# Routing by one-hot products on chip, laid inside the output projection, in an encoder layer with grouped experts

## The chip, the core and the metric

The kernel runs on one core of one Trainium2 chip. The metric is the device time of one launch in microseconds (us). Beside five engines (TensorE or PE, VectorE or DVE, ScalarE or ACT, GpSimd or POOL, SyncE or SP) the core has 16 DMA engines. SP's transfers go through one queue (q1), those that GpSimd issues, gathers and scatters by index among them, through another (q0); both use the same 16 DMA engines.

## The reference, cut to what matters

There are 768 tokens (512 and 256) of 1024 channels. A token mixer (latent attention with 4 heads beside pooling over windows) ends in a product with `w_out`; then each token goes to two of eight experts in one of four groups.

```
h = x + concat(attention, pooling) @ w_out
a = rmsnorm(h) * g_ffn
group = argmax(a @ w_group_router + b_group_router)       # 4 groups
e1, e2 = top2 of (a @ w_expert_router + b_expert_router) in that group
gate = softmax value of the group * normalised top-2 softmax values
y = h + sum over e in (e1, e2) of gate_e * (silu(a @ w_gate[e]) * (a @ w_up[e])) @ w_down[e]
```

All is float32. The 32 experts have 3 MB of weights each (1024x256, 1024x256, 256x1024), 96 MB in all, and each is read once.

## The kernel before

The program is written by hand: each engine has its own list of instructions, in the order of the code, and they meet at semaphores.

1. **Projections**, tile by tile (128 tokens, six tiles). The weights come in at the start on SP's queue, large ones first, then ten small ones (the list `small`: rotary tables, the two router matrices, broadcast gains), a slot table, two tables of zeros, and the third and fourth tile of x. DVE waits for all ten small ones (`gains_in`) ahead of the rotary tables of tile 0 (line 1065).
2. **Attention and pooling.**
3. **Output projection and routing.** For tile i, PE makes two halves of `h` (`out_half`, 24 products of 128x512 in each, lines 476 to 481). DVE adds x (line 1166). ACT squares, POOL takes the root, DVE writes the normalised row times the gain into `rows` (line 1174). PE turns the row round (`row_transposes`, line 712) and multiplies it with the router (`logits`, line 720) after the second half of the *next* tile. DVE finds the group and two experts as one-hot rows (`route`), PE counts how many earlier tokens chose each expert (`ranks`), DVE turns the counts into a place in the slot table (`positions`), and POOL writes the token's number there by an indirect DMA into memory (line 1390, two for each tile). The gates are columns 1024 to 1055 of the token's row in the table `token_rows`.
4. **Experts.** Expert j and expert 16+j form a pair; each has 64 lanes, the two halves of 128 partitions. For each of 16 pairs POOL gathers 128 rows of `token_rows` by the slot table (line 1413), PE turns them round (line 754), multiplies with gate and up weights (line 767) and with down weights (line 783), and POOL adds the 128 results to `out` (line 1432). Unused slots name a row of zeros beyond the 768. Where an expert has more than 64 tokens an *over pass* follows the pair, with its own gather (`more_rows`).

The weights of a pair come in six parts of 1 MB (gate, up, down for two lanes) into one of three buffers, on SP's queue, at most three parts under way. Part 0 to 3 of pair j are issued once PE has done gate and up of pair j-3 and of its over passes (`refill`), parts 4 and 5 once the down products are done. Ahead of the expert stage pair 0 is loaded during the output projection. Of pair 1 four parts are issued around the last tile; the other two, and pair 2, wait for the first gather (`sp.wait_ge(main.gathered[0], 16)`). The first gather waits for the slot table, which is read back (lines 426 to 429) once all 12 scatters have landed.

With the inputs of this case the experts get 1536 assignments. 1533 of the 2048 slots of the first passes are used (of pairs 0, 1 and 2 it is 110, 108 and 117 of 128); pair 0 and pair 6 have an over pass, with one and two tokens in its 128 slots. This is worked out from the reference and its inputs.

## Time and profile before

| | us |
|---|---|
| median of 3 runs | 644.66 (644.41 to 644.89) |
| the profiled execution, its own time | 643.67 |
| its span | 642.0 |
| TensorE busy | 530.8 (83% of the span) |
| VectorE, ScalarE, GpSimd busy | 223.6, 147.0, 133.2 |
| SP's queue q1 | 128.60 MB |
| GpSimd's queue q0 | 19.72 MB |

An execution is the span plus 1.7 us outside it. Line numbers in rows are those of the listing above. "PEld" is TensorE's weight load, beside PE. A row of the chain of waits is a piece of work that was followed by what waited for it; in a timeline the last bracket is how long the engine stood idle ahead of the row and what released it.

### The profile page before, as it was taken

To read this page: it belongs to the slowest core of one execution; us is meant where nothing else is said; L and a number is where in the kernel's file an instruction comes from. 1 tells how busy PE (TensorE), PEld (TensorE's weight loads), DVE (VectorE), ACT (ScalarE), POOL (GpSimd) and SP (SyncE) were. 2 spreads that over 40 slices of the span, in tenths; PEclk is the share of its full clock that TensorE was granted. 3 is DMA by queue.
4 is the path that set the end of the run, shared out by engine and by line. 5 is a ranking of instruction groups with operands and counts; after the bars stand their busy time and mean duration, and the time that the engine had idled before them with its cause. 6 is when DMAs were issued, how large, how long until landed. Compare 5 with 4: busy or idle time off the path is not lost.

```text
span 642.0 us, 8839 instructions
## 1 busy us (share of the span) xinstructions
PE 530.8 (83%) x3092; PEld 373.3 (58%) x3093; DVE 223.6 (35%) x602; ACT 147.0 (23%) x310; POOL 133.2 (21%) x200
## 2 busy tenths in 40 slices
PE   5889999997898989999725877989788897777762
PEld 4768988884444568888624545555445564434430
DVE  4743335225959562566650211121211211111110
ACT  6734343322546221121201101010100100000000
POOL 0122232032244000034323102111201232011110
PEclk9999999999999999999856989799989999889997
DMA  8730100000620039243467999999999999999992
GB/s 333 240 142 35 32 2 1 1 0 1 236 72 27 2 137 387 100 132 133 171 227 253 405 374 388 392 367 379 388 393 390 392 392 379 403 390 392 388 363 34
DMA packets 31163, 148.81 MB, mean 232 GB/s; under 512 B 7139, under 2 KB 7798, under 8 KB 18822
## 3 DMA queue, kind: packets, MB, share of 16 engines
q1 hardware_dynamic: 25376, 128.60, 50.2%
q0 software_dynamic: 5712, 19.72, 11.7%
q8 instruction: 22, 0.36, 0.2%
q14 instruction: 15, 0.12, 0.1%
q10 hardware_dynamic: 38, 0.01, 0.0%
HBM read 132.48 MB, written 17.00 MB: 233 GB/s over the span
## 4 chain that ended last, share of the span: by engine, by line
DMA 45%; PE 25%; issue 10%; DVE 6%; POOL 4%; ACT 1%; POOLq 0%; SPq 0%
DMA expert_w<-in_w_down 25%; DMA expert_w<-in_w_up 19%; PE ps L476 4%; PE ps L477 4%; PE ps L481 4%; PE ps L641 3%; POOL slot_tokens L1390 2%; PE ps L582 2%; DVE p_sb L1130 2%; PE ps L596 2%; PE ps L599 1%; PE ps L628 1%; PE ps L516 1%; DMA g_rows<-token_rows,idx_now 1%; PE ps L667 1%
## 5 line engine op out<-in xcount | busy, mean ns | idle before, releaser
L767 PE MATMUL ps<-expert_w,xT 128*64 128x256 f32 x1152 | 132.2, 386 | 16.4 <-DMA expert_w<-in_w_up 6.8
L767 PEld LDWEIGHTS ps<-expert_w,xT 128*64 128x64 f32 x1152 | 97.7, 140 | 55.5 <-issue 27.8
L783 PE MATMUL ps<-expert_w,hT 128*64 128x512 f32 x288 | 76.8, 681 | 23.7 <-DMA expert_w<-in_w_down 13.2
L1432 POOL DMA_INDIRECT out<-y_sb,idx_now x18 | 28.7, 1593 | 202.6 <-DVE y_sb L1302 201.8
L783 PEld LDWEIGHTS ps<-expert_w,hT 128*64 128x64 f32 x288 | 25.5, 155 | 63.1 <-issue 60.7
L1290 DVE SCALAR_TENSOR_TENSOR hid<-s_act,gate,ps 128x256 f32<-128x256 f32 x18 | 11.9, 660 | 141.5 <-ACT s_act L968 141.5
L476 PE MATMUL ps<-w_in_hi,aT_hi 128*128 128x384 f32 (+2 forms) x120 | 43.7, 368 | 0.0
L1302 DVE COPY y_sb<-ps 128x512 f32<-128x512 f32 x18 | 12.5, 692 | 89.5 <-PE ps L783 89.5
L477 PE MATMUL ps<-w_in_lo,aT_hi 128*128 128x384 f32 (+2 forms) x120 | 40.8, 344 | 0.0
L968 ACT ACTIVATE s_act<-ps 128x256 f32<-128x256 f32 x18 | 6.9, 384 | 133.7 <-PE ps L767 133.7
L973 ACT ACTIVATE y_sb<-ps 128x512 f32<-128x512 f32 x18 | 10.8, 597 | 105.6 <-PE ps L783 105.6
L754 PE MATMUL ps<-consts_sb,g_rows 128*128 128x128 f32 x128 | 18.4, 289 | 15.3 <-DMA g_rows<-token_rows,idx_now 15.3
L754 PEld LDWEIGHTS ps<-consts_sb,g_rows 128*128 128x128 f32 x128 | 14.4, 146 | 21.3 <-DMA g_rows<-token_rows,idx_now 16.3
L1381 POOL TENSOR_TENSOR w_out_lo<-w_out_raw,w_out_hi 128x1024 fp32r<-128x1024 f32 x8 | 19.0, 2378 | 34.1 <-ACT w_out_hi L920 34.1
L481 PE MATMUL ps<-w_in_hi,aT_lo 128*128 128x384 f32 (+2 forms) x120 | 24.3, 344 | 0.0
L477 PEld LDWEIGHTS ps<-w_in_lo,aT_hi 128*128 128x128 f32 x120 | 22.6, 188 | 2.6 <-issue 1.2
L476 PEld LDWEIGHTS ps<-w_in_hi,aT_hi 128*128 128x128 f32 x120 | 22.6, 188 | 2.6 <-issue 1.2
L582 PE MATMUL ps<-w_ukv_sb,cT_kv 128*128 128x512 f32 x48 | 21.6, 592 | 0.0
L481 PEld LDWEIGHTS ps<-w_in_hi,aT_lo 128*128 128x128 f32 x120 | 20.6, 188 | 1.6
L1390 POOL DMA_INDIRECT slot_tokens<-tok_ids,idx_pos x12 | 18.7, 1556 | 10.9 <-DVE m_sum L1246 8.3
L596 PE MATMUL ps<-kT,qT 128*128 128x512 f32 (+1 forms) x48 | 20.2, 545 | 0.8 <-DVE rT L1106 0.8
L1413 POOL DMA_INDIRECT g_rows<-token_rows,idx_now x17 | 17.1, 1004 | 14.4 <-POOL idx_now L1424 13.5
(205 smaller groups left out, 856.5 us busy)
## 6 DMA issues: line engine op xcount, KB each, us to landing
expert_w<-in_w_gate SPq DMA_DIRECT2D x32, 1024.0 KB, 9.7
expert_w<-in_w_up SPq DMA_DIRECT2D x32, 1024.0 KB, 8.5
expert_w<-in_w_down SPq DMA_DIRECT2D x32, 1024.0 KB, 10.4
w_in_raw<-in_w_in SPq DMA_DIRECT2D x8, 608.0 KB, 10.3
w_out_raw<-in_w_out SPq DMA_DIRECT2D x8, 512.0 KB, 3.6
token_rows<-rows SPq DMA_DIRECT2D x6, 528.0 KB, 3.4
out<-h_sb SPq DMA_DIRECT2D x6, 512.0 KB, 2.9
x_sb<-in_x_prompt SPq DMA_DIRECT2D x4, 512.0 KB, 9.9
```

What stands on the lines that cost most here:

```text
L476: pe.matmul(dst, l_hi(k), r_hi(k), start=(first and k == ks[0]), stop=False)
L477: pe.matmul(dst, l_hi(k), r_lo(k), start=False, stop=False)
L481: mm = pe.matmul(dst, l_lo(k), r_hi(k), start=False, stop=(last and k == ks[-1]))
L582: mm = pe.matmul(ps[:, 5 + n, :], cT_kv[:, k, :], w_ukv[:, k, n * 512:(n + 1) * 512], start=(k == 0), stop=(k == KKV - 1))
L596: pe.matmul(ps[:, bank + u, 0:n], qT[:, h, q], kT[:, h, keys], start=True, stop=False)
L641: mm = pe.matmul(ps[:, 6 + u, 0:SEQS[s]], v_sb[:, FIRST[s] + c, h * DV:(h + 1) * DV], pT[:, u, c, 0:SEQS[s]], start=(c == 0), stop=(c == T ...
L754: mm = pe.transpose(ps[:, banks + k // 4, (k % 4) * P:(k % 4 + 1) * P], src[:, k * P:(k + 1) * P], ident)
L767: mm = pe.matmul(ps[r, 2, g * FH:(g + 1) * FH], xT[:, q.o, k, r], w_gu(b, lane, k, g), start=(k == 0), stop=(k == KD - 1))
L783: mm = pe.matmul(ps[r, 4 + half, :], hT[:, q.o, k, r], w_dn(b, lane, k, half), start=(k == 0), stop=(k == 1))
L1381: pool.tensor_tensor(w_out_lo[:, k, :], w_out_raw[k % 3][:, :], w_out_hi[:, k, :].bitcast(F32), ALU.subtract).then_inc(w_out_lo_done, 1)
L1390: pool.indirect_dma_start(out=slot_table, out_offset=bass.IndirectOffsetOnAxis(ap=idx_pos[:, i, c:c + 1], axis=0), in_=tok_ids[:, i:i + 1] ...
L1432: pool.indirect_dma_start(out=out, out_offset=bass.IndirectOffsetOnAxis(ap=idx, axis=0), in_=y_sb[:, buf, :], in_offset=None, compute_op=A ...
```

## The change

- **Slot table on chip.** For each tile, DVE builds two one-hot matrices `slot_a` (token by lane), and ACT two matrices `slot_b` (token by expert: the one-hot row times the token's number, and times its gate). PE adds their products up over the six tiles in one bank (`slots`). DVE copies the sum out as the indices of the first passes (`idx_all`) and as the gates (`gate_all`). The table in memory is still written by 12 scatters, but it is read for the over passes alone (`idx_more`), by a transfer that POOL issues.
- **Rows and gates apart.** `token_rows` has 1024 columns; the gates go to a table `token_gates`. An over pass gathers from both.
- **Gathers with a bound.** `token_rows` has 768 rows and none of zeros. Unused slots name a row beyond the end, and the gather has `bounds_check=T - 1, oob_is_err=False`.
- **Logits from `h`.** PE turns round `h_sb`, not `rows`; the gain is multiplied into the router's weights at the start, and the reciprocal root into the logits on DVE. The router's weights and the gain come in another layout (`(k p)` for `(p k)`).
- **Order.** The output projection is cut in four parts for each tile, with transposes, logits and slot products between them. The normalised row of the last tile is made by ACT and POOL.
- **SP.** The other parts of pair 1, and pair 2, do not wait for the first gather.

```
 small = [ ...
-    (w_router[:, :, 0:EG], a["w_group_router"][0].rearrange("(p k) n -> p k n", k=KD)),
+    (w_router[:, :, 0:EG], a["w_group_router"][0].rearrange("(k p) n -> p k n", k=KD)),
...
+    (g_router[:, :], a["g_ffn_norm"][0].rearrange("(k p) -> p k", k=KD)),
...
-sp.dma_start(table[T:T + P, :], a["zeros"]).then_inc(setup_dram, 16)
...
 for i in range(NT):                                   # SP
     sp.wait_ge(h_done, 2 * (i + 1))
...
     else:
-        load_pair(sp, 1, 1, range(3))
+        load_pair(sp, 1, 1, range(2))
     if i >= 1:
         store_rows(i - 1)
-load_pair(sp, 1, 1, range(3, 4))
+    if i >= 2:
+        store_gates(i - 2)
 store_rows(NT - 1)
-sp.wait_ge(slots_stored, 2 * NT * 16)
-sp.wait_ge(counts_done, 1)
-sp.dma_start(idx_all[:, 0:PAIRS], slot_table[0:BLOCK, :] ...).then_inc(idx_in, 16)
...
-sp.wait_ge(main.gathered[0], 16)
+store_gates(NT - 2)
+load_pair(sp, 1, 1, range(2, 4))
+store_gates(NT - 1)
 load_pair(sp, 1, 1, range(4, 6))
 load_pair(sp, 2, 2)
...
+def slots(i):                                         # PE
+    pe.wait_ge(slot_a_done, i + 1)
+    pe.wait_ge(slot_b_done, 2 * (i + 1))
+    for c in range(2):
+        mm = pe.matmul(ps[:, 5, 0:2 * E], slot_a[:, c, :], slot_b[:, c, :], start=(i == 0 and c == 0),
+                       stop=(i == NT - 1 and c == 1))
...
 for i in range(NT):                                   # PE
-    out_half(i, 0)
-    if i >= 1: row_transposes(i - 1)
-    out_half(i, 1)
-    if i >= 2: ranks(i - 2)
-    if i >= 1: logits(i - 1)
+    out_part(i, 0, False)
+    if i >= 1: h_transposes(i - 1, 1)
+    out_part(i, 0, True)
+    if i >= 1: logits(i - 1, 0); logits(i - 1, 1)
+    if i >= 2: slots(i - 2)
+    out_part(i, 1, False)
+    h_transposes(i, 0)
+    out_part(i, 1, True)
+    if i >= 1: ranks(i - 1)
...
+dve.tensor_tensor(w_router[:, :, :], w_router[:, :, :],            # DVE, tile 0 of the projections
+                  g_router[:, :].unsqueeze(2).to_broadcast([P, KD, EG + E]), ALU.mult).then_inc(tables_set, 1)
...
 route(NT - 1)                                         # DVE
 route_weights(NT - 1)
+slot_of(NT - 1)
+table_place(NT - 1)
+dve.wait_ge(slot_mm, NT)
+for lane in range(2):
+    r = slice(lane * LANE, (lane + 1) * LANE)
+    dve.tensor_scalar(idx_all[r, 0:PAIRS], ps[r, 5, PAIRS * lane:PAIRS * (lane + 1)], spare_row[r], None,
+                      ALU.add).then_inc(idx_done, 1)
...
+pool.wait_ge(last_scaled, 1)                          # POOL
+pool.wait_ge(rows_stored, 16 * (last - 1))
+pool.tensor_tensor(rows ... , h_junk ... , g_ffn ... , ALU.mult).then_inc(a2_done, 1)
 fill_slots(NT - 2)
-fill_slots(NT - 1)
-pool.wait_ge(idx_in, 16)
+pool.wait_ge(idx_done, 3)
 pool.wait_ge(rows_stored, 16 * NT)
 pool.wait_ge(h_stored, 16 * NT)
...
+    pool.indirect_dma_start(out=dst, out_offset=None, in_=src, in_offset=bass.IndirectOffsetOnAxis(ap=idx, axis=0),
+                            bounds_check=T - 1, oob_is_err=False).then_inc(done, 16)
...
-gather_pair(0, 0, 1)
-pool.wait_ge(idx_rest_in, 32)
+gather(g_rows[:, 0, :], table, idx_all[:, 0:1], main.gathered[0])
+gather(g_rows[:, 1, :], table, idx_all[:, 1:2], main.gathered[1])
+fill_slots(NT - 1)
+pool.wait_ge(slots_stored, 2 * NT * 16)
+pool.dma_start(idx_more[:, :], slot_table[BLOCK:2 * BLOCK, :] ...).then_inc(idx_rest_in, 16)
+pool.wait_ge(counts_done, 1)
+pool.wait_ge(gates_stored, 16 * NT)
+pool.wait_ge(idx_rest_in, 16)
 first_more_gather(0)
-gather_pair(1, 1, 2)
```

The order on PE from the last products of the output projection to the first gathered rows, before:

```order
L481 MATMUL ps<-w_out_hi,pool_lo 128x512 x4
L728 MATMUL ps<-m_sum,bf_consts 128x32
L729 MATMUL ps<-m_sum,bf_consts 128x32
L720 MATMUL ps<-w_router,a2T 128x36 x8
L712 MATMUL ps<-consts_sb,rows 128x128 x8
L728 MATMUL ps<-m_sum,bf_consts 128x32
L729 MATMUL ps<-m_sum,bf_consts 128x32
L720 MATMUL ps<-w_router,a2T 128x36 x8
L728 MATMUL ps<-m_sum,bf_consts 128x32
L729 MATMUL ps<-m_sum,bf_consts 128x32
L745 MATMUL ps<-m_sum,bf_consts 128x32
```

And in the changed kernel, where L727 turns `h_sb` round, L738 are the logits, L755 the slot products and L781 the totals:

```order
L493 MATMUL ps<-w_out_hi,pool_lo 128x512 x4
L747 MATMUL ps<-m_sum,bf_consts 128x32
L748 MATMUL ps<-m_sum,bf_consts 128x32
L738 MATMUL ps<-w_router,a2T 128x36 x4
L727 MATMUL ps<-consts_sb,h_sb 128x128 x4
L738 MATMUL ps<-w_router,a2T 128x36 x4
L755 MATMUL ps<-slot_b,slot_a 128x64 x2
L747 MATMUL ps<-m_sum,bf_consts 128x32
L748 MATMUL ps<-m_sum,bf_consts 128x32
L755 MATMUL ps<-slot_b,slot_a 128x64 x2
L781 MATMUL ps<-m_sum,bf_consts 128x32
L790 MATMUL ps<-consts_sb,g_rows 128x128 x8
```

Half of the last tile's transposes and the logits of tile 4 now stand ahead of these rows, between the products; four slot products are new.

The order on SP around the last store of `h` (L415), before:

```order
L411 DMA token_rows<-rows 128x1056
L415 DMA out<-h_sb 128x1024
L266 DMA expert_w<-in_w_gate 128x2048 x2
L266 DMA expert_w<-in_w_up 128x2048
L411 DMA token_rows<-rows 128x1056
L266 DMA expert_w<-in_w_up 128x2048
L411 DMA token_rows<-rows 128x1056
L426 DMA idx_all<-slot_tokens 128x16
L427 DMA idx_more<-slot_tokens 128x16
L429 DMA idx_all<-in_slots 128x1
L266 DMA expert_w<-in_w_down 128x2048 x2
L266 DMA expert_w<-in_w_gate 128x2048 x2
```

And in the changed kernel, with L430 the store of `h`, L420 the rows, L426 the gates and L273 the weights:

```order
L426 DMA token_gates<-gate_rows 128x32
L430 DMA out<-h_sb 128x1024
L273 DMA expert_w<-in_w_gate 128x2048 x2
L420 DMA token_rows<-rows 128x1024
L426 DMA token_gates<-gate_rows 128x32
L420 DMA token_rows<-rows 128x1024
L426 DMA token_gates<-gate_rows 128x32
L273 DMA expert_w<-in_w_up 128x2048 x2
L426 DMA token_gates<-gate_rows 128x32
L273 DMA expert_w<-in_w_down 128x2048 x2
L273 DMA expert_w<-in_w_gate 128x2048 x2
```

Two parts of pair 1 have moved behind the store of the last tile's rows, and nothing stands between the last gates and the parts that follow.

The order on POOL from the last scatters to the first gathers, before:

```order
L1400 TENSOR_TENSOR route_f<-route_f,neg_half 128x1
L1390 DMA slot_tokens<-tok_ids,idx_pos 24576x1 x6
L1424 COPY idx_now<-idx_all 128x1
L1413 DMA g_rows<-token_rows,idx_now 128x1056
L1448 TENSOR_LOAD counts_i
L1448 ISA x2
L1449 COMPARE_AND_BRANCH
L1450 COPY idx_now<-idx_more 128x1
L1451 ISA
L1453 REGISTER_ALU
L1413 DMA more_rows<-token_rows,idx_now 128x1056
```

And in the changed kernel, where L1501 are the scatters into the slot table, L1517 the last tile's rows, L1528 the gathers and L1619 the reading of `idx_more`:

```order
L1517 TENSOR_TENSOR rows<-h_junk,g_ffn 128x1024
L1501 DMA slot_tokens<-tok_ids,idx_pos 24576x1 x2
L1528 DMA g_rows<-token_rows,idx_all 128x1024 x2
L1501 DMA slot_tokens<-tok_ids,idx_pos 24576x1 x2
L1619 DMA idx_more<-slot_tokens 128x16
L1567 TENSOR_LOAD counts_i
L1567 ISA x2
L1568 COMPARE_AND_BRANCH
L1569 COPY idx_now<-idx_more 128x1
L1570 ISA
L1572 REGISTER_ALU
L1528 DMA more_rows<-token_rows,idx_now 128x1024
```

Both first gathers now stand ahead of the last two scatters, and the over pass's gathers behind these and behind L1619.

## Rows read from the trace of the kernel before

**Rows 1.** The page, its chain that ended last: shares of the span by line.
```profile
DMA expert_w<-in_w_down 25%; DMA expert_w<-in_w_up 19%; PE ps L476 4%; PE ps L477 4%; PE ps L481 4%; PE ps L641 3%; POOL slot_tokens L1390 2%; PE ps L582 2%; DVE p_sb L1130 2%; PE ps L596 2%; PE ps L599 1%; PE ps L628 1%; PE ps L516 1%; DMA g_rows<-token_rows,idx_now 1%; PE ps L667 1%
```

**Rows 2.** The chain of waits, 315 to 642 us: start, us, piece.
```profile
338.32 4.33 DMA g_rows<-token_rows,idx_now
...
343.04 11.90 DMA expert_w<-in_w_down
...
362.39 9.87 DMA expert_w<-in_w_down
...
616.38 9.84 DMA expert_w<-in_w_down
```

**Rows 3.** Windows, the expert stage: busy us (count), granted clock, DMA share, GB/s.
```profile
342.00:626.00 284.00, 230.64 (x1604) 141.66 (x1604) 45.67 (x107) 29.11 (x54) 50.40 (x66) 0.94 1.01 384
```

**Rows 4.** DMA queues, 342 to 627 us: packets, MB, share of sixteen engines.
```profile
q1 hardware_dynamic: 12384, 90.18, 76.3%
q0 software_dynamic: 5056, 18.67, 24.4%
```

**Rows 5.** Timeline of SyncE's queue: start, us, line, transfer.
```profile
314.94 0.86 SPq L266 DMA_DIRECT2D expert_w<-in_w_gate  x2
...
342.67 0.80 SPq L266 DMA_DIRECT2D expert_w<-in_w_down  x2
...
370.09 0.89 SPq L266 DMA_DIRECT2D expert_w<-in_w_gate  x2
```

**Rows 6.** Timeline of the over pass, TensorE: start, us.
```profile
360.12 1.09 PE L754 MATMUL ps<-consts_sb,more_rows 128*128 128x128 f32 x8
```

**Rows 7.** Timeline of TensorE in one output-projection tile, and its end.
```profile
293.14 1.04 PE L712 MATMUL ps<-consts_sb,rows 128*128 128x128 f32 x8
293.94 0.48 PE L476 MATMUL ps<-w_out_hi,o_hi 128*128 128x512 f32 x1
...
299.56 1.95 PE L720 MATMUL ps<-w_router,a2T 128*128 128x36 f32 x16
301.34 0.48 PE L476 MATMUL ps<-w_out_hi,o_hi 128*128 128x512 f32 x1
```

**Rows 8.** Timeline of VectorE: the last addition of the residual.
```profile
313.43 0.69 DVE L1166 TENSOR_TENSOR h_sb<-ps,x_res 128x512 f32<-128x512 f32 x1 [4.27 <-PE ps L481]
```

**Rows 9.** Timeline of VectorE: routing of the last tile, first and last.
```profile
325.12 0.16 DVE L1187 TENSOR_TENSOR route_f<-ps,r_bias 128x4 f32<-128x4 f32 x1 [1.12 <-PE ps L720]
...
327.94 0.19 DVE L1208 TENSOR_TENSOR m_sum<-route_f 128x32 bf16<-128x32 f32 x1
```

**Rows 10.** Timeline of GpSimd, 316 us; then a line group of the page.
```profile
316.46 2.62 POOL L1390 DMA_INDIRECT slot_tokens<-tok_ids,idx_pos  x1 [0.20 <-issue]
...
L1381 POOL TENSOR_TENSOR w_out_lo<-w_out_raw,w_out_hi 128x1024 fp32r<-128x1024 f32 x8 | 19.0, 2378 | 34.1 <-ACT w_out_hi L920 34.1
```

**Rows 11.** DMA issues: scatters from 319 us, gathers from 341 us, to landing.
```profile
slot_tokens<-tok_ids,idx_pos POOLq DMA_INDIRECT x2, 8.1
...
g_rows<-token_rows,idx_now POOLq DMA_INDIRECT x1, 9.5
```

**Rows 12.** The tile view of g_rows, the time from issue to landing.
```profile
DMA to landing us min/median/max: 4.3/11.2/13.0
```

**Rows 13.** Timeline of the first tile: what DVE, ACT and PE waited for.
```profile
36.83 1.43 DVE L1065 TENSOR_TENSOR rope_tab<-rope_tab,q_x 128x256 f32<-128x256 f32 x4 [5.09 <-DMA q_x<-in_g_k_head]
...
41.81 1.06 ACT L823 ACTIVATE u_sb<-x_sb 128x1024 f32<-128x1024 f32 x1 [8.30 <-DMA x_sb<-in_x_prompt]
...
41.83 0.66 PE L516 MATMUL ps<-consts_sb,q_n 128*128 128x128 f32 x4 [1.57 <-DVE q_n L1084]
...
47.13 0.63 PE L516 MATMUL ps<-consts_sb,k_n 128*128 128x128 f32 x4 [1.13 <-DVE k_n L1097]
```

**Rows 14.** DMA packets in 24 to 27.4 us, then in 27.4 to 36.5 us.
```profile
DMA packets 2298, 0.50 MB, mean 148 GB/s; under 512 B 2211, under 2 KB 2211, under 8 KB 2298
...
DMA packets 932, 0.63 MB, mean 69 GB/s; under 512 B 906, under 2 KB 906, under 8 KB 920
```

391 lines of the change are left out of this document (237 added, 154 removed).

## The prediction

> **What bounds the kernel now.** I read the page's chain first. Its shares by line put 44% of the span on two transfers of expert weights [rows 1]; no engine comes near. The chain in order of time shows where: from 343.04 to 626.22 us it is nothing but weights, 30 pieces of 7 to 12 us [rows 2], and what is left is one pair's down products, its copy and its addition into `out`. In that stage the 16 DMA engines are busy for a share of 1.01, while TensorE is busy 230.6 of 284 us [rows 3]. So a microsecond of PE's there is worth nothing. What counts is when the stream of weights runs without a gap, and how many bytes it shares its engines with: SP's queue takes 76.3% of them and GpSimd's, with a sixth of the bytes, 24.4% [rows 4].
>
> SP's queue says when the stream runs [rows 5]. Pair 1's early parts go out from 314.94, then nothing goes until 342.67, when the first gather has landed. The next stop is pair 3: its first part goes out at 370.09, as soon as PE has done gate and up of pair 0's over pass, which began with its transposes at 360.12 [rows 5, 6]. The last part of pair 2 lands at 372.26 (362.39 + 9.87 [rows 2]), so the hand-over just fits, with 2.2 us of transfers still queued. From there on no gap is seen. The end is thus set by two numbers, the restart at pair 3 and the time per byte behind it.
>
> **The change, part by part.**
>
> *The start.* A gain table of 1024 elements of 4 B joins the small loads, ahead of the broadcasts for which DVE waits until 36.83; PE's first query transposes stand 1.57 us idle behind that, so any delay counts [rows 13]. The two router matrices and a small table are 2298 packets, moved in 3.4 us [rows 14]: 1024 packets at that pace are 1.5 us. DVE's new product over 288 columns takes 0.4 (the nearest row, 256 columns, is a quarter of 1.43 us) [rows 13]. Against it, a table of zeros is gone (528 KB, 1.3 us at the stage's 384 GB/s [rows 3]) ahead of the x tile for which ACT stood until 41.81, and the key transposes lose up to 1.1 us of waiting [rows 13]. Query path +1.9, less 1.1, and 0.5 for one more issue (0.4 each [rows 5]): +1.3 us. Bounds: -0.5 (packets free) and +11 (below). That a full stage of PE follows makes it all pass on.
>
> *The output projection.* PE is full there, so I count its work up to the last product, T, which the last addition puts at 313.4 [rows 8]. The logits of tile 4 now stand ahead of T instead of behind it: 1.8 us (from 299.56 to the next product at 301.34) [rows 7]. Half of one more set of transposes does too: 0.4 (293.14 to 293.94, halved) [rows 7]. Slot products for tiles 0 to 3 are new, two each; one logit product of eight is 0.22, so 4 x 0.45 = 1.8. T becomes 313.4 + 4.0 + 1.3 = 318.7. The other engines have room: DVE gets some eight more small operations a tile (1.6 us), and it stood idle for 4.27 us ahead of the last addition [rows 8]. If that cover went, up to 1.6 us for each of five tiles would show.
>
> *From T to the first gather.* DVE first finishes tile 4 (slot, place and gate, 19 operations of about 0.2 us: from 325.12 to 327.94 there are 17 instructions [rows 9]): T+4.3. The route of tile 5 takes 3.0 to the mask and 1.0 behind it, its slot 1.6, PE's product and the places another 2, the copy of indices 0.6: T+12. POOL writes the last rows in between (2.4 us by the line of the same size [rows 10], up to 4 with its strides), behind two scatters (each 1 to 2.6 [rows 10]). SP stores them at about T+9, behind 3.1 MB of other transfers issued from T+1, which last 8 us: they land at T+13. The first gather goes out at T+13.5. Before, it took 4.33 us on idle engines [rows 2]; now parts 2 and 3 of pair 1 are in flight. A gather beside weights took 9.5, and the median of all 17 is 11.2 [rows 11, 12]. I take 10: it lands at T+23.5 = 342.2 against 342.67. Bounds: T+18 and T+25.
>
> The Trainium skill ("DMA: Bandwidth & Descriptors", Queues, rings and completion order) says that a DMA engine's semaphore write lands only after every earlier write of that engine, across its queues. By that rule a small gather pays for the weights in flight beside it, as 4.33 against 9.5 shows [rows 2, 11]; by the size alone it would land at T+18.
>
> *The over pass of pair 0.* Before, its indices lay ready. Now POOL issues the last two scatters behind the gathers (T+15.6 to T+18), and they land about 8 us after issue beside weights (8.1 in the row [rows 11]): T+24. Then `idx_more` comes by POOL's queue, another 8: T+32. Then two gathers, T+34.5 with their issue, and some 7 to land (5 to 9.5): T+41.5. PE wants them 17.4 us after the first gather (342.67 to 360.12 [rows 6]): T+41. They meet. Behind POOL's new waits stand the gather of pair 2 and the first addition into `out`, which nobody needs before PE is through with pair 0. Ten microseconds later (360.12 to 370.09) SP may issue pair 3: T+51.5 = 370.2, against 370.09.
>
> *The stream ahead of that.* Parts 2 and 3 leave at T+10 and nothing gates the other eight parts, so the stream's bytes up to pair 3 would be through 9 us earlier than before. But pair 3 has no buffer until PE lets go of pair 0. So the head start runs into a gap of about 8 us, T+43 to T+53.5, and the restart is where it was: 372.3 then, 372.2 now. Net +0.1. Bounds: -6 (first gather at T+18, over pass in time) and +5 (each hop 11 us; once the stream has dried, hops are short).
>
> *Behind the restart.* Unused slots named real rows of zeros; now their index lies beyond the bound. If the engines move nothing for them, of pairs 3 to 15 466 rows go and of pair 6's over pass 126: 592 rows of 4224 B, 2.5 MB. At SP's pace (76.3% of 285 us for 90.18 MB, 2.4 us per MB [rows 4]) that is 6.0 us, at GpSimd's own (3.7 us per MB [rows 4]) 9. The queue is full throughout, so it is all saved. I take 6.0, since the additions, which read and write, raise the second figure. Bounds: 0 and 9. That rows shrink from 4224 to 4096 B is 0.3 us at most. Gates no longer taken out of the rows are DVE work off the path.
>
> *Sum.* Against the profiled execution's own 643.67: 0.1 - 6.0 = 637.8. The runs' median is 1.0 above that execution: 638.8.
>
> **Rivals.**
>
> *A. The head start is kept.* Gathers land soon (4.3 to 5 us) and the over pass finds its rows when PE wants them. Pair 3 then goes out at T+45.4, 6 us earlier: 633. For it: three small DMAs at a time share 16 engines and most of the load is one queue. Against: 9.5 beside weights [rows 11].
>
> *B. Dropped rows cost what they did.* The DMA engines, or GpSimd's descriptors, do the same work for an index beyond the bound. No row here shows such a gather. Then 6.0 falls away: 645.
>
> *C. The over pass is late.* Each of its four hops takes 11 us, and PE stands 5 us for its rows, under which pair 3 waits: 644. For it: the median of 11.2 [rows 12]. Against: the stream is dry by the last hop.
>
> *D. The small loads are slow (slower than before).* The broadcasts behind the router's loads moved at most 906 packets in 9.1 us, where the router's took 1.5 ns each [rows 14]. If the gain table's 1024 packets go at the broadcasts' pace of 10 to 12 ns, the first tile starts 11 us later instead of 1.5, and everything with it: 648. It decides from about 9 us of delay, where the 6.0 is used up. For it: packets of 4 B have no row here. Against: the router's, of 1024 short pieces each and with the same 128 partitions on the slow side, are what it resembles.
>
> The Trainium skill (same page, Why a DMA increments its semaphore by 16 and not by 1) says that a copy runs on as many engines, up to 16, as divide the slowest dimension of both sides. Here that is 128, so all 16 would work and D would not come; the difference of pace in the trace does not contradict that [rows 14], and by that rule I leave D little.
>
> **How the numbers follow.** Forecast (rows dropped, hand-over at the old time) 0.42, time 639, own range 635 to 642. A 0.18. B 0.22. C 0.08. D 0.10. No change is what lies within 0.2% (1.3 us) of 644.66, about what a measurement of this kernel can tell. Faster: nearly all of the forecast (0.41), all of A (0.18), of B a quarter (0.055), of C 0.03: 0.68. Slower: half of B less a little (0.08), of C 0.01, D 0.10, and 0.01 of the rest: 0.20. Same: 0.12. The range reaches from A's time to D's, 633 to 648, and leaves out A with a long gain and D with a full one.
>
> **What would show it.** Right: T near 318.7; `g_rows` landing at 340 to 344; a gap in SP's weights between pair 2 and pair 3 with the DMA share falling near 362 to 372, ended by PE's gate and up of the over pass; then q0 with some 590 packets of 4 KB fewer and the last weights at about 620. Wrong: q0 with as many row packets as before (B); the first query transposes later than 45 us (D); no gap and pair 3 issued before 366 (A); PE waiting over 3 us for `more_rows` (C). Beside these, a PE that idles between tiles in the output projection would undo the count to T.

## The result

The changed kernel is slower. Its median is 651.15 us (648.93 to 653.51, four runs) against 644.77 us for the kernel before on the same chip (644.41 to 645.68, four runs); the ratio is 1.0093, with an interval of 1.0063 to 1.0124. The forecast was 639 us, with a range up to 648, and a chance of 0.20 for slower. The profiled execution took 648.93 us with a span of 647.3, where 643.67 and 642.0 stood before.

Three points in time divide the whole run, and the rest of this text goes by them: T (the last product of the output projection, read from the last addition of the residual), the issue of pair 3's first weights, and the last weights in (the last down products). Each comes from the profiled execution of its kernel. The changed kernel's first and third mark, and the third mark of before, in the chain of waits (start, us, piece):

```profile
320.36 0.70 DVE h_sb L1241
...
630.94 3.67 PE ps L819 x16
```
```profile
626.31 3.67 PE ps L783 x16
```

| | last addition | from there to pair 3 | from pair 3 to the last weights in |
|---|---|---|---|
| before | 313.43 | 56.7 | 256.2 |
| forecast | 318.7 | 51.5 | 250.2 |
| changed | 320.36 | 58.4 | 252.2 |

The forecast let T come later and the restart at pair 3 stay where it was, so its second column is 5 us shorter than before. The three errors are +1.7, +6.9 and +2.0, together 10.6 of the 11.1 us between the profiled execution and the 637.8 forecast for it. That execution was the fastest of the four, 2.2 us below their median, so 12.3 us lie between the median and the forecast's 638.8, and the marks cannot account for more than what one execution shows. The third column is 256.2 less the 6.0 that the dropped rows should have been worth.

### The profile page after: what moved, and what is told of

The parts are those of the page before. It is cut to its first block, busy times and chain, and to the rows that moved or that the text cites. A ratio compares the mean times of both kernels' runs of the same rounds, so it can differ in the third digit from the quotient of the medians.

```text
span 647.3 us, 8990 instructions
## 1 busy us (share of the span) xinstructions
PE 533.7 (82%) x3116; PEld 376.8 (58%) x3117; DVE 226.4 (35%) x633; ACT 156.6 (24%) x347; POOL 138.8 (21%) x202
## 3 DMA queue, kind: packets, MB, share of 16 engines
q0 software_dynamic: 5808, 15.75, 10.3%
## 4 chain that ended last, share of the span: by engine, by line
DMA 46%; PE 38%; DVE 5%; SPq 5%; issue 3%; POOL 2%; ACT 0%; POOLq 0%
DMA expert_w<-in_w_down 21%; DMA expert_w<-in_w_up 18%; PE ps L488 7%; PE ps L489 7%; PE ps L493 7%; SPq L382 3%; PE ps L653 3%; PE ps L594 2%; PE ps L608 2%; DMA slot_tokens<-tok_ids,idx_pos 2%; DMA q_x<-in_g_k_head 1%; DMA x_res<-in_x_prompt 1%; PE ps L803 1%; PE ps L611 1%; PE ps L738 1%
## 5 line engine op out<-in xcount | busy, mean ns | idle before, releaser
L803 PE MATMUL ps<-expert_w,xT 128*64 128x256 f32 x1152 | 134.8, 391 | 17.4 <-DMA expert_w<-in_w_up 7.3
L803 PEld LDWEIGHTS ps<-expert_w,xT 128*64 128x64 f32 x1152 | 99.3, 141 | 57.5 <-issue 29.7
L819 PE MATMUL ps<-expert_w,hT 128*64 128x512 f32 x288 | 71.7, 642 | 21.0 <-DMA expert_w<-in_w_down 13.2
L819 PEld LDWEIGHTS ps<-expert_w,hT 128*64 128x64 f32 x288 | 24.2, 147 | 56.6 <-issue 56.6
L1507 POOL TENSOR_SCALAR route_f<-route_f 128x1 f32<-128x1 f32 x6 | 2.0, 338 | 93.7 <-ACT h_junk L983 93.7
L488 PE MATMUL ps<-w_out_hi,pool_hi 128*128 128x512 f32 x48 | 19.9, 415 | 0.4 <-DVE pool_lo L1221 0.4
```

Source lines behind the costliest of these rows:

```text
L488: pe.matmul(dst, l_hi(k), r_hi(k), start=(first and k == ks[0]), stop=False)
L803: mm = pe.matmul(ps[r, 2, g * FH:(g + 1) * FH], xT[:, q.o, k, r], w_gu(b, lane, k, g), start=(k == 0), stop=(k == KD - 1))
L819: mm = pe.matmul(ps[r, 4 + half, :], hT[:, q.o, k, r], w_dn(b, lane, k, half), start=(k == 0), stop=(k == 1))
```

## The profile after

The page's queues and its chain, where [rows 1] has 44% of the span on expert weights of `down` and `up`, and here 39%: columns are packets, MB and share of sixteen engines, then shares of the chain.

```profile
q1 hardware_dynamic: 26704, 128.08, 50.5%
q0 software_dynamic: 5808, 15.75, 10.3%
...
DMA expert_w<-in_w_down 21%; DMA expert_w<-in_w_up 18%; PE ps L488 7%; PE ps L489 7%; PE ps L493 7%; SPq L382 3%; PE ps L653 3%; PE ps L594 2%; PE ps L608 2%; DMA slot_tokens<-tok_ids,idx_pos 2%; DMA q_x<-in_g_k_head 1%; DMA x_res<-in_x_prompt 1%; PE ps L803 1%; PE ps L611 1%; PE ps L738 1%
```

GpSimd's queue q0 is down to 15.75 MB: the skip works. What is new in the chain is the transfer of a scatter into `slot_tokens` (only its issue stood there before) and the start (`SPq L382`, the small loads).

The first tile, answering to [rows 13]: start, us, and in brackets what the engine stood idle for. The first line is SyncE's issue of the gain table.

```profile
19.76 7.14 SPq L382 DMA_DIRECT2D g_router<-in_g_ffn_norm  x1
...
38.79 1.43 DVE L1137 TENSOR_TENSOR rope_tab<-rope_tab,q_x 128x256 f32<-128x256 f32 x4 [7.07 <-DMA q_x<-in_g_k_head]
40.25 0.46 DVE L1140 TENSOR_TENSOR w_router<-w_router,g_router 128x288 f32<-128x288 f32 x1
...
44.16 0.66 PE L528 MATMUL ps<-consts_sb,q_n 128*128 128x128 f32 x4 [3.89 <-DVE q_n L1158]
```

The rope table starts 1.96 us later than at 36.83, the new product takes 0.46, and the query transposes start 2.3 us later than at 41.83. TensorE stood 3.89 us for them instead of 1.57. The 7.14 us of SyncE's queue are not the gain table's: in the kernel before, the transfer at the same place stood just as long,

```profile
19.78 8.16 SPq L374 DMA_DIRECT2D q_x<-in_g_q_head  x3
```

so one more issue pushed the last broadcasts back by 0.5 us only (28.51 against 27.98). The next view shows what followed: windows of 44 to 52 us and two more (columns as in [rows 3]: after the busy times come granted clock, DMA share, GB/s).

```profile
44.00:52.00 8.00, 7.84 (x40) 7.49 (x41) 3.54 (x12) 3.50 (x11) 3.22 (x8) 0.79 0.00 1
...
366.00:372.00 6.00, 4.58 (x21) 3.23 (x23) 0.99 (x3) 0.60 (x1) 1.31 (x1) 0.53 0.74 152
372.00:380.00 8.00, 6.72 (x56) 4.35 (x52) 0.66 (x1) 0.38 (x1) 0.00 (x0) 0.92 0.07 10
```

The same windows of the kernel before:

```profile
44.00:52.00 8.00, 6.87 (x38) 5.86 (x37) 3.01 (x11) 3.59 (x12) 4.09 (x10) 1.00 0.00 1
...
366.00:372.00 6.00, 4.17 (x38) 2.82 (x34) 1.08 (x2) 0.38 (x1) 0.00 (x0) 1.00 0.99 292
372.00:380.00 8.00, 6.52 (x28) 2.77 (x30) 0.69 (x1) 0.60 (x1) 0.93 (x1) 0.79 1.00 417
```

Two things stand there. Behind the longer wait the granted clock is 0.79 in 44 to 52 us, a mixture of the full level (2.4 GHz) and the lower one (1.2 GHz), while TensorE is busy for 7.84 of the 8 us: some 1.7 us (8 x 0.21, an estimate) of full-speed work is not done. And between pair 2 and pair 3 the engines of the DMA stand idle for 6 x 0.26 + 8 x 0.93 = 9.0 us, where the kernel before loses 0.1.

TensorE's new slot products, on the other hand, are what they were thought to be. In one tile they stand between the logits and the next product for 0.44 us (285.16 to 285.60):

```profile
285.16 0.64 PE L755 MATMUL ps<-slot_b,slot_a 128*128 128x64 f32 x4
285.60 0.48 PE L488 MATMUL ps<-w_out_hi,o_hi 128*128 128x512 f32 x1
```

The gap ahead of pair 3 was forecast, at about 8 us. What was not is that it ends so late. SyncE's queue around it, answering to [rows 5]:

```profile
321.47 1.25 SPq L273 DMA_DIRECT2D expert_w<-in_w_gate  x2
322.81 0.44 SPq L420 DMA_DIRECT2D token_rows<-rows  x1
323.35 0.52 SPq L426 DMA_DIRECT2D token_gates<-gate_rows  x1
333.85 0.32 SPq L420 DMA_DIRECT2D token_rows<-rows  x1
334.26 0.38 SPq L426 DMA_DIRECT2D token_gates<-gate_rows  x1
...
378.73 0.90 SPq L273 DMA_DIRECT2D expert_w<-in_w_gate  x2
```

The last tile's rows leave at 333.85. Yet GpSimd had them ready at 328.34, as its timeline shows, beside the one operation of VectorE's routing that ran next to it:

```profile
325.48 2.86 POOL L1517 TENSOR_TENSOR rows<-h_junk,g_ffn 128x1024 f32<-128x1024 f32 x1
```
```profile
325.50 2.87 DVE L1273 TENSOR_SCALAR route_f<-consts_sb,route_f 128x4 f32<-128x4 f32 x1
```

SyncE's waits say what it stood for (total us, times, longest):

```profile
SPq L459 <- PE ps L803: 21.3, 2, 18.2
...
SPq L419 <- DMA token_rows<-rows: 9.9, 1, 9.9
```

The second of these is the miss. Before it may store the last rows, SyncE waits until the rows of the tile before have landed, and these were issued right behind the first 2 MB of pair 1's weights. It stood for 9.9 us, the last 5.5 of them with the rows ready (333.85 less 328.34). The kernel before has no such wait ahead of its stores: there SyncE waits for the rows and gates alone. It came with the change. From there the chain of waits runs like this (start, us, piece):

```profile
337.63 1.07 POOL g_rows L1528
...
341.64 9.89 DMA slot_tokens<-tok_ids,idx_pos
...
351.82 5.78 DMA idx_more<-slot_tokens
...
359.89 1.07 POOL more_rows L1528
...
361.26 5.24 DMA more_gate<-token_gates,idx_now
366.55 1.98 PE ps L790 x8
...
369.39 9.01 PE ps L803 x64
```

The first gather leaves 17.3 us behind T instead of the forecast's 13.5. Its transposes start at 346.48, by TensorE's timeline,

```profile
346.48 1.97 PE L790 MATMUL ps<-consts_sb,g_rows 128*128 128x128 f32 x8 [12.59 <-DMA g_rows<-token_rows,idx_all]
```

so it took 8.9 us where 4.33 stood in [rows 2] and 10 were forecast, and landed 2.7 us behind the forecast's T+23.5. The last scatters land at T+31.2 (forecast T+24), TensorE gets the over pass's rows and gates at T+46.2 (T+41.5) and is through at T+58.1 (T+51.5). The last step holds a second fall of the clock: gate and up of the over pass took 9.01 us, behind a wait of 2.57 us. The granted clock was 0.53 in 366 to 372 and 0.92 in 372 to 380, and 0.79 over these 9.01 us themselves.

## The experiments

Each kernel was compared with the kernel before on the same chip. That kernel's median was 645.70, 645.66 and 645.48 in the three comparisons; its single runs spread from 641.9 to 650.8, so the time of one run says less than the marks in its trace. The marks in turn are those of one execution. Those of the changed kernel are from the shortest of its four runs, twice, and those of "scatters first" and "all four" from long ones, so the medians and the marks can put a single edit up to 3.5 us apart. The marks of all profiled executions are in a table behind the experiments. "Changed" is the kernel with the change; a second comparison of it, as it is, gave 652.66, ratio 1.0135 (1.0080 to 1.0190).

> The changed kernel itself, as the measure for the others of this call: 649 to 653, pair 3 issued near 378.7, a gap in the weights of some 10 us ahead of it.

### What the dropped rows are worth

Changed, with the table of zeros back and the bound behind it:

```diff
-    table = nc.dram_tensor("token_rows", [T, D], F32, kind="Internal").ap()
+    table = nc.dram_tensor("token_rows", [T + P, D], F32, kind="Internal").ap()
+            sp.dma_start(table[T:T + P, :], a["zeros"]).then_inc(setup_dram, 16)
-                                        bounds_check=T - 1, oob_is_err=False).then_inc(done, 16)
+                                        bounds_check=(T + P - 1 if src is table else T - 1), oob_is_err=False).then_inc(done, 16)
```

> The changed kernel, but its row table has the 128 rows of zeros again and the gathers' bound takes them in, so that each unused slot moves a row. The zeros are stored behind the x loads, so the start is not touched. Theory (dropped rows save DMA time behind the restart at pair 3; the stream there was 3.9 us shorter than before): 4 to 6 us slower than the changed kernel, pair 3 issued within 2 us of 378.7, GpSimd's queue about 3.2 MB more. Rival (the shorter stream comes from something else, dropped rows save nothing): within 1 us.

Measured: 655.75 us, ratio 1.0173 (1.0104 to 1.0243). From pair 3 to the last weights it took 257.1 us, against 252.2 and 253.0 in the two traces of the changed kernel. The queues in exactly this stretch, first with zero rows (380.4 to 637.5 us), then the changed kernel in its second comparison (378 to 631 us):

```profile
DMA packets 15740, 98.21 MB, mean 382 GB/s; under 512 B 1776, under 2 KB 1776, under 8 KB 5744
...
q1 hardware_dynamic: 11232, 81.79, 77.0%
q0 software_dynamic: 4496, 16.26, 23.9%
```
```profile
DMA packets 15740, 95.26 MB, mean 377 GB/s; under 512 B 2498, under 2 KB 2498, under 8 KB 5744
...
q1 hardware_dynamic: 11232, 81.79, 79.1%
q0 software_dynamic: 4496, 13.30, 21.8%
```

The same number of packets goes in both, but 722 of them have become small (2498 less 1776), and 2.96 MB are gone. GpSimd's queue saves 23.9% of 257.1 less 21.8% of 253.0, 6.3 us. The weights, the same 81.79 MB, cost 79.1% of 253.0 instead of 77.0% of 257.1, which is 2.1 us more. What is left, 4.2 us, is the 4.1 us by which the stretch is shorter. This is why the term of 6.0 came out near 4. The bytes dropped were more than forecast, 2.96 MB for 2.5: there are 17 gathers of first passes and not 16 [rows 12], and the last one names nothing but unused slots, 128 rows that the forecast's 592 leave out (592 and 128 are 720 of the 722). But the packets of the weights took longer beside fewer others, so that a dropped MB was worth 1.4 us (4.1 by 2.96) and not 2.4. The two errors partly cancel. Rival B is out.

The kernel before, with a bound that drops its rows of zeros:

```diff
-                                        in_offset=bass.IndirectOffsetOnAxis(ap=idx, axis=0)).then_inc(done, 16)
+                                        in_offset=bass.IndirectOffsetOnAxis(ap=idx, axis=0),
+                                        bounds_check=T - 1, oob_is_err=False).then_inc(done, 16)
```

> The kernel before with one edit: its gathers carry the bound of 768 rows, so rows for unused slots are not moved. Theory (saving is the stream's, and nothing else of the change is needed for it): 4 to 7 us faster than before, 638 to 641, pair 3 still issued at 370, the last weights at 620 to 622. Rival (the check makes each gather dearer, or the saving needs the change's own order): within 1 us of before.

Measured: 641.60 us, ratio 0.9942 (0.9921 to 0.9963). This one line is a gain alone, of 4.1 us by the medians and 3.3 by the stretch (252.9 against 256.2), less than the 4 to 7 expected.

### The over passes

Changed, with the counts of over passes shifted to zero, and SyncE's wait for them gone. It leaves out 3 of the 1536 assignments, those beyond an expert's 64 slots:

```diff
-                    sp.wait_ge(kind(over), passes)
-            dve.tensor_scalar(counts_i[0:1, 3, :], counts_i[0:1, 0, :], 6, None, ALU.arith_shift_right).then_inc(counts_done, 1)
+            dve.tensor_scalar(counts_i[0:1, 3, :], counts_i[0:1, 0, :], 31, None, ALU.arith_shift_right).then_inc(counts_done, 1)
```

> The changed kernel without over passes: their number is set to zero, so three of 1536 assignments are left out of the result. Theory (the gap in the weights between pair 2 and pair 3, 366 to 380, is the wait for pair 0's over pass): pair 3 is issued when PE has done pair 0, near 358, there is no gap, and the kernel is 12 to 15 us faster than the changed one, 634 to 638. Rival (the gap has another cause, such as the late first gather, or PE is the bound behind it): under 6 us faster.

Measured: 633.91 us, ratio 0.9830 (0.9783 to 0.9877), 17 us below the changed kernel's first median, more than was expected. Pair 3 goes out 39.6 us behind the last addition instead of 58.4, there is no gap (DMA share 1.03 and 1.02 in 366 to 372 and 372 to 380 us), and the last weights are in at 614.72. But over passes also have a price of their own, so the same edit was made to the kernel before:

> The kernel before without over passes (three of 1536 assignments are left out). Theory (there the over pass of pair 0 ended just when the stream was ready for pair 3, so it cost nothing): within 3 us of before, the 2 us being the two gathers and additions that go. Rival (the over pass held the kernel before too): 6 us or more faster.

Measured: 635.67 us, ratio 0.9878 (0.9832 to 0.9925). The expectation was too low by far: nearly 10 us by the medians, the rival's size. In the profiled executions the last weights are in 11.0 us earlier, of which 3.4 are a last addition that came earlier (310.02), in a part that the edit does not touch; the stretch from there to the last weights is shorter by 7.6 us. q0 carries 17.59 MB instead of 19.72, and 2.13 MB at GpSimd's own 3.7 us per MB (from [rows 4]) are 7.9 us, so its transfers are enough for that. In the changed kernel the same stretch is shorter by 17.3 us for 1.06 MB (14.69 against 15.75), some 4 us by the same rate. What is left, about 13 us, is what the late over pass costs the changed kernel, head start included. The share of each is worked out from a rate, and not measured apart.

### The order of the last scatters and the first gathers

Changed, with the last two scatters ahead of the first gathers on GpSimd:

```diff
+            fill_slots(NT - 1)
             pool.wait_ge(idx_done, 3)
             ...
-            fill_slots(NT - 1)
```

> The changed kernel, with the last two scatters into the slot table issued ahead of the first two gathers instead of behind them. Theory (the over pass of pair 0 waits for the chain of scatters, idx_more and its own gathers, and pair 3 waits for it): more_rows lands 4 to 6 us earlier, PE's wait of 2.6 us for it goes, pair 3 is issued 2 to 4 us earlier and the kernel is 2 to 4 us faster. Rival (the first gather's late landing at 346.5 alone sets the hand-over): PE's wait goes but nothing else, at most 2 us; if the gathers are pushed back by the scatters, no gain.

Measured: 646.62 us, ratio 1.0008 (0.9978 to 1.0038), where the changed kernel has 1.0093 and 1.0135; the 2 to 4 us expected are seen in the marks (2.6), and more by the medians. Its over pass, on TensorE:

```profile
366.21 1.09 PE L790 MATMUL ps<-consts_sb,more_rows 128*128 128x128 f32 x8
368.70 7.13 PE L803 MATMUL ps<-expert_w,xT 128*64 128x256 f32 x64 [1.41 <-DVE xT L1387]
```

No wait stands in front of `more_rows` (TensorE itself comes there later, as the first gather did), the granted clock is 1.00 in 366 to 372 us, and gate and up take 7.13 us instead of 9.01. The rows come at the same time as before the edit (366.2 against 366.5), for the first gather was 1.3 us later here (347.81 against 346.48); of the 2.6 us by which pair 3 is earlier (376.18), 2.2 lie behind the rows' arrival, of which the clock makes the larger part: 1.9 in gate and up.

### The wait of SyncE

Changed, with the rows of the tile before the last, and the gates of the one before that, stored ahead of the first 2 MB of pair 1's weights:

```diff
-                else:
-                    load_pair(sp, 1, 1, range(2))
                 if i >= 1:
                     store_rows(i - 1)
                 if i >= 2:
                     store_gates(i - 2)
+                if i + 1 == NT:
+                    load_pair(sp, 1, 1, range(2))
```

> The changed kernel, with the fifth tile's rows and fourth tile's gates stored ahead of the first two parts of pair 1 on SP's queue, not behind. Theory (the last tile's rows were stored 5 us late, at 333.85, since SP waited 9.9 us for the fifth's to land behind 2 MB of weights): the last rows are stored near 329, the first gather goes out 2 to 3 us earlier, near 335, bounded then by the indices at 334.4, and the kernel is 2 to 3 us faster. Rival (the first gather only lands later beside more weights): no gain.

Measured: 646.29 us, ratio 1.0019 (0.9997 to 1.0042), 6.4 us below the changed kernel of the same comparison; the last weights are in 2.9 us earlier. One of its ten runs took 1731.12 us; I have no reason for it, and the median does not feel it. SyncE's queue:

```profile
322.31 0.38 SPq L420 DMA_DIRECT2D token_rows<-rows  x1
322.78 0.74 SPq L426 DMA_DIRECT2D token_gates<-gate_rows  x1
323.57 1.69 SPq L273 DMA_DIRECT2D expert_w<-in_w_gate  x2
329.15 0.33 SPq L420 DMA_DIRECT2D token_rows<-rows  x1
```

The last rows leave at 329.15, 8.0 us behind the last addition, where it was 13.5. No wait stands there now but that for the rows. The first gather gains less, for now it waits for VectorE's indices and gates: it goes out at 336.20, 15.0 behind the last addition instead of 17.3. Pair 3 is at 54.5 instead of 58.4: 2.2 us of it by the gather's issue, 0.6 by the hops behind it (TensorE has the over pass's rows and gates at 364.53), and 1.0 behind that, where the clock fell less (0.72 in 366 to 372 us).

### The gain table

Changed, with the router's gains loaded behind the x tiles, and multiplied in when the output projection begins:

```diff
-                (g_router[:, :], a["g_ffn_norm"][0].rearrange("(k p) -> p k", k=KD)),
+                sp.dma_start(g_router[:, :], a["g_ffn_norm"][0].rearrange("(k p) -> p k", k=KD)).then_inc(g_router_in, 16)
```

> The changed kernel, with the gain table loaded behind all x tiles and multiplied into the router's weights only ahead of the output projection. Theory (this load and product cost the start 2.3 us): first query transposes at 41.8 to 42.3 instead of 44.16, everything behind 1.5 to 2.5 us earlier. Rival (the start is limited by the x tile for which ACT waits): under 0.5 us.

Measured: 647.18 us, ratio 1.0026 (1.0000 to 1.0053), 5.5 us below the changed kernel of the same comparison. TensorE's first query transposes, and the windows of 44 to 52 us (TensorE alone):

```profile
41.35 0.66 PE L529 MATMUL ps<-consts_sb,q_n 128*128 128x128 f32 x4 [1.59 <-DVE q_n L1157]
```
```profile
44.00:52.00 8.00, 8.00 (x46) 1.00 0.00 1
```

The start is back (41.35, wait 1.59 as before), the gain table's issue, now at 76.00, takes 0.43 us, the clock stays up, and the last addition is at 316.05, 4.5 us earlier than in the changed kernel's second trace (320.59), though the transposes are only 2.3 earlier. The clock's 1.7 us are most of the 2.2 us between the two. One pair of traces is not enough for the size: three kernels load the table late, with a last addition at 314.36, 316.05 and 319.27, and eight load it early, at 319.72 to 321.51. The means are 4.2 us apart. That this table costs some 4 us at T, and not the 2.4 forecast for it (1.5, 0.4 and 0.5), is the first error. Every kernel here with the table among the first loads shows the same: a wait of 3.53 to 4.25 us and a granted clock of 0.67 to 0.83 in 44 to 52 us, eight traces out of eight.

### The head start

Changed, with SyncE's weights held from the fifth part of pair 1 on until the first gather has landed:

```diff
+            sp.wait_ge(main.gathered[0], 16)
             load_pair(sp, 1, 1, range(4, 6))
```

> The changed kernel, with the wait of the kernel before put back: the last two parts of pair 1, and pair 2, are issued only once the first gather has landed. Theory (weights in flight slow each hop of the scatters, the index list and the gathers, and the head start is worth nothing as pair 3 waits for the over pass): the first gather lands 2 to 4 us earlier, the over pass finds its rows, pair 3 is issued at 370 to 374, and the kernel is 4 to 8 us faster for doing less ahead. Rival (the head start counts): 3 to 6 us slower.

Measured: 645.78 us, ratio 1.0009 (0.9977 to 1.0040), 6.9 us below the changed kernel of the same comparison. SyncE's queue and TensorE's over pass:

```profile
336.15 0.33 SPq L426 DMA_DIRECT2D token_gates<-gate_rows  x1
342.90 0.81 SPq L273 DMA_DIRECT2D expert_w<-in_w_down  x2
```
```profile
361.96 1.09 PE L791 MATMUL ps<-consts_sb,more_rows 128*128 128x128 f32 x8 [0.41 <-DMA more_gate<-token_gates,idx_now]
363.97 7.13 PE L804 MATMUL ps<-expert_w,xT 128*64 128x256 f32 x64 [0.92 <-DVE xT L1388]
```

The weights leave 5.6 us later than in the changed kernel (337.30), and everything behind is earlier. The first gather leaves where it did (T+17.2) but lands in 5.92 us by the chain of waits instead of 8.9. The over pass waits 0.41 instead of 2.57 us and runs at full clock. Pair 3 goes out 51.7 us behind the last addition instead of 58.4 and, in the second trace, 57.4. The head start was worth less than nothing: pair 3 had no buffer for what it gave, and what it took were the hops.

The same gather thus took 4.33 us on idle engines [rows 2], 5.92 behind 2 MB of weights, and 8.9 where the next parts had begun to leave 0.3 us ahead of it (337.30 against 337.63). The Trainium skill ("DMA: Bandwidth & Descriptors", Queues, rings and completion order) has a completion wait for the earlier writes of each engine; by that rule the weights ahead would count, and the trace agrees as far as these three go. They do not part it from a plain sharing of the sixteen engines.

### The last tile's rows on VectorE

Changed, with the last tile's rows on VectorE like the others, so that GpSimd's 2.86 us operation is gone:

```diff
-                if i + 1 < NT:
-                    second_norm(i)
+                second_norm(i)
```

> The changed kernel, but the last tile's normalised row is made by VectorE in one instruction behind tile 4's gates, as for the other tiles, not by ScalarE and GpSimd. Theory (GpSimd's 2.86 us instruction on that row holds up VectorE, whose compare of four columns beside it took 2.87 us instead of 0.23): the compare takes 0.23, VectorE pays 2.1 for the row, so the indices come 0.5 us earlier or the same and the kernel changes by under 1 us. Rival (the compare was long for another reason): it stays long and the indices come 2 us later.

Measured: 649.75 us, ratio 1.0082 (1.0049 to 1.0115), which its interval does not part from the changed kernel's. VectorE, with the operation on the rows and the one that had taken 2.87 us:

```profile
325.52 1.96 DVE L1243 SCALAR_TENSOR_TENSOR rows<-h_sb,route_f,g_ffn 128x1024 f32<-128x1024 f32 x1
...
328.44 0.27 DVE L1268 TENSOR_SCALAR route_f<-consts_sb,route_f 128x4 f32<-128x4 f32 x1
```

The 128x4 comparison is down from 2.87 to 0.27 us. In all ten traces in which GpSimd's operation runs, it starts within 0.04 us of it and takes 2.86 or 2.87 us; the same line took 0.23 us for the tile before. So it was that operation that held it. By which way the one holds the other no run here shows. But VectorE pays 1.96 for the rows instead, so the indices are ready only 0.9 us earlier behind T (334.66 less 321.51, against 334.41 less 320.36), and the first gather waits for SyncE's store anyway, which again leaves late, at 333.65.

### The edits together

Two kernels join edits from above: scatters first, rows first and gains late; and the same with the hold.

> The same as the run with four edits, but without the hold: the later parts of pairs 1 and 2 go out at once. Theory (weights in flight slow the first gather and the list of the over pass): first gather lands 3 to 5 us later than with the hold, pair 3 is issued 3 to 5 us later, and the kernel is 3 to 5 us slower than with it. Rival (with the scatters early the hops no longer stand beside weights): within 1 us of each other.

> The changed kernel with four edits tried singly: the last scatters ahead of the first gathers, the fifth tile's rows stored ahead of the weights, the gain table loaded late, and the later parts of pairs 1 and 2 held until the first gather has landed. Theory (each takes away a hop or a delay of one chain, from the start over the last rows and the first gather to pair 3): last product near 316, first gather issued near 331.5 and landed near 336.5, pair 3 issued 27 us later at 363 to 366, execution 634 to 638, faster than both kernels. Rival (the chain has another member of the same length, or the stream is not ready at 364): 639 to 644.

Measured: 641.76 us, ratio 0.9954 (0.9932 to 0.9977), and with the hold 638.85 us, ratio 0.9893 (0.9849 to 0.9937). The second beats both kernels. That it comes out at the 639 forecast for the change is chance: it is another kernel, and it missed the 634 to 638 expected of it, as its first gather took 6.9 us (335.34 to 342.28) and not 5. The hold is worth 2.9 us here by the medians and 3.9 up to pair 3 (50.8 against 54.7), about the 3 to 5 expected and less than the 6.9 it gave alone: with the scatters early, what is left of it is the first gather (9.9 us without the hold), and TensorE does not wait for the over pass's rows in either. SyncE's queue and the over pass of the kernel with all four:

```profile
370.09 0.90 SPq L273 DMA_DIRECT2D expert_w<-in_w_gate  x2
```
```profile
360.13 1.09 PE L792 MATMUL ps<-consts_sb,more_rows 128*128 128x128 f32 x8
```

Both marks are where they stood before the change, within 0.01 us [rows 5, 6], though the last addition came 5.8 us later, and the dropped rows are then kept: the last weights are in at 622.61 instead of 626.31. Its profiled execution was the slowest of its four runs (641.68), with a clock of 0.79 in 38 to 46 us and the last addition at 319.27, though TensorE had waited only 1.84 us; what made the clock fall there stays open.

### All marks

| kernel | last addition | to pair 3 | pair 3 to last weights | DMA share 366–372, 372–380 |
|---|---|---|---|---|
| before | 313.43 | 56.7 | 256.2 | 0.99, 1.00 |
| before, bound alone | 311.09 | 57.2 | 252.9 | 0.58, 1.01 |
| before, no over passes | 310.02 | 51.2 | 254.1 | 1.01, 1.03 |
| changed | 320.36 | 58.4 | 252.2 | 0.74, 0.07 |
| changed, second trace | 320.59 | 57.4 | 253.0 | 0.58, 0.15 |
| zero rows read | 320.75 | 59.7 | 257.1 | 0.91, 0.02 |
| no over passes | 321.41 | 39.6 | 253.8 | 1.03, 1.02 |
| scatters first | 320.52 | 55.7 | 252.9 | 0.57, 0.52 |
| rows first | 321.16 | 54.5 | 252.5 | 0.61, 0.40 |
| gains late | 316.05 | 57.8 | 253.3 | 0.03, 0.64 |
| hold | 319.72 | 51.7 | 252.4 | 0.69, 0.95 |
| rows on VectorE | 321.51 | 55.5 | 253.4 | 0.60, 0.24 |
| three together | 314.36 | 54.7 | 252.5 | 0.36, 1.01 |
| all four | 319.27 | 50.8 | 252.5 | 0.43, 0.99 |

The columns move apart: the gains act on the first, the order of hops and the hold on the second, the bound on the third alone. One kernel's marks differ by about 1 us between two traces (changed, twice), and the first column by up to 3.4 among the three kernels of before and 4.9 among the three with late gains, which do not differ ahead of it. So the first column is read by groups and not by single traces: 311.5 in the mean of the three of before, 320.8 of the eight with early gains, 316.6 of the three with late ones. By these means the start and the output projection cost 9.2 us, where the table of marks has 6.9, because 313.43 was the latest of before's kind.

## Why the prediction was wrong

**What bounds the kernel: right.** The stream of weights sets the end in every kernel, and its restart at pair 3 is the place that counts.

**The start: right in kind, too small.** The +1.3 was 2.4 at the query transposes (1.5 for packets, 0.5 for an issue, 0.4 for the product) less 1.1 at the key transposes. Measured are 2.3 at the query transposes, with 1.96 at the rope table for 2.0 and 0.46 for the product, and the key transposes' wait of 1.13 us is gone. These terms came out. What the sum lacks is the clock, whose fall behind the longer wait adds some 1.7. What failed is that a wait on TensorE was counted at its length, when the work behind it also runs slower. Rival D had the sign and the place, but not the size of 11 us.

**The output projection: right.** Slot products stand for 0.44 us in each tile (285.16 to 285.60) against 0.45; the gains-late kernel, whose query transposes start about where they did before, reaches its last addition 2.6 us later than before. By the forecast's terms it should be 2.9 (4.0 less the 1.1 of the key transposes), so the 4.0 stands, within what the column scatters.

**From T to the first gather: the step that failed.** The forecast has SyncE store the last rows "at about T+9, behind 3.1 MB of other transfers". It did so at T+13.5, because, with the rows ready at T+8.0, it first waited for the landing of the rows before them, which lay behind 2 MB of weights. I had priced the transfers in front of this store, but not the wait ahead of it on the same queue. The rows-first kernel shows that the wait was the cause of the late store, and that 2.2 of the gather's 3.8 us go with it. Behind it VectorE's indices are next, at 15.0 us. That is a second miss under the first: the indices and gates were forecast for T+12 and ready at T+14.5, and 2.6 of it is the comparison that GpSimd's operation on the last rows held (2.87 us for 0.23).

**The over pass: right in its chain, too fast in its hops.** "They meet", at T+41 and T+41.5, became T+46.2; from first issue to TensorE the four hops cost 28.9 us (337.63 to 366.55) against 28.0, so it was the late beginning that counted (3.8 us), and then 2.2 us from the rows to pair 3 (12.2 for 10.0), behind the wait, at the lower clock. That is rival C's mechanism, a TensorE that stands for its rows, at 2.57 us instead of the 5 that were its condition, and with the late beginning (3.8) and 0.9 of slower hops it made 6.9 us, more than the +5 that I had set as the bound of the hand-over. That bound was made of slow hops alone; no wait on SyncE and no lower clock stood in it.

**The head start: worse than nothing.** "Net +0.1" and rival A both took its transfers as free. The hold shows that they cost 6.7 us between the last addition and pair 3 (5.7 against the second trace), and 3.9 beside the other edits. This is no fourth error on top of the three: part of the slow hops was forecast, and the hold makes up for the late beginning by quick ones. So its 51.7 at pair 3 is near the forecast's 51.5 by chance.

**The dropped rows: right in kind, but half as large again as measured.** 6.0 was forecast, 4.1 measured between kernels that differ in nothing else, and 3.3 in the kernel before. The rate used (one queue's bytes into its share of the engines) takes for granted that the other queue's packets stay as they are; they got 2.1 us slower in all. The bytes were too low by a gather of 128 unused rows, which hid part of this: with 2.96 MB the same rate gives 7.1 us.

**The sum.** 1.7 + 6.9 + 2.0 = 10.6 us. Without the middle one the profiled execution would have been 642.0, 1.7 below before's, and the median (651.15 less 6.9) 644.3, no faster than before. So the middle error made the kernel slower, but the other two had already used up nearly all of the gain. The range to 648 had room for the middle one alone, not for all three.

## What to carry to other kernels

When work is moved into a stretch that was waiting, follow the queue that issues it past every wait that stands ahead of it, not only past the bytes. A transfer that starts early is a gain only where it has a buffer and where nobody short is behind it: here holding the weights back by 5.6 us, until a small gather had landed, gave 6.9 us, and 2.9 in the kernel with the other edits. And separate the edits of a change: the one line with a bound was worth 4.1 us alone, and it was buried under 10 us that came from its company.

## What the runs showed of the hardware

- An indirect gather with an index beyond its bound moves no row, but leaves a small packet: 722 row packets became packets under 512 B, and 2.96 MB went.
- After a wait of 3.5 to 4.3 us on TensorE at the start, the granted clock was 0.67 to 0.83 in 44 to 52 us, in eight traces of eight; behind waits of 0.4 to 1.6 us it was 1.00, in five of five. With one of 1.84 us it was 0.90, and 0.79 in 38 to 46 us.
- Gate and up of the first over pass, 64 products, took 7.13 us at a granted clock of 1.00 behind waits of 0 to 0.41 us for its rows (six traces of six), and 8.46 to 9.01 us behind waits of 0.92 to 3.82 (six of six); the 9.01 were at 0.79.
- A VectorE comparison of 128x4 took 2.87 us beside GpSimd's 2.86 us operation on 128x1024, and 0.27 without it; 2.86 or 2.87 in ten traces of ten with it.
- One load of 1024 elements of 4 B took SyncE 0.43 us to issue at 76.00 us, in the gains-late kernel, and 7.14 at 19.76, behind the two router matrices; there the transfer in its place took 8.16 in the kernel before, too.
